# The end of the sample tile: gating ahead of the norm factor, new homes for squares and factors, new orders on three engines

## Chip, cores and metric

One core of one Trainium2 chip runs the whole program. The metric is the device time of one execution in microseconds (us), lower is better.

## The reference, cut to what matters

Two layers of a hybrid encoder run over 512 prompt tokens and 8 x 16 sample tokens with shared weights. The first layer's mixer holds four gated-DeltaNet heads and four mLSTM heads. This case is about how the outputs of the eight heads are finished and about the states of the sample sequences:

```python
o_a = o_a * lax.rsqrt(jnp.mean(o_a * o_a, axis=-1, keepdims=True) + EPS) * gdn_norm_w
o_a = o_a * jax.nn.silu(z_a)
h_b = h_b * lax.rsqrt(jnp.mean(h_b * h_b, axis=-1, keepdims=True) + EPS)
h_b = h_b * mlstm_norm_w * jax.nn.sigmoid(o_b)
out = jnp.concatenate([o_a, h_b], axis=-1) @ w_out
S = exp(gL) * S + k_end^T u            # per sequence and gated-DeltaNet head, an output
C = decay * C + kw^T v ;  n = decay * n + sum(kw)    # per sequence and mLSTM head, outputs
```

The factor of a head is 1/root of the mean of its squared output, so it has to be taken from the output before the gate (silu or sigmoid) is applied.

## The kernel before, in words

Features lie on the 128 partitions and all T = 640 tokens (512 prompt, 128 sample) on the free axis. fp32 products are made of three fp32r products, high x high, low x high and high x low, so each weight block is loaded to `raw` by SyncE, rounded to `whi` by ScalarE (`prep`) and its rest `wlo` is made by GpSimd (`low`). The mixer's core walks over five token tiles; the first four belong to the prompt, the fifth is the sample tile. Every engine has its own instruction order written out by hand, and engines meet at semaphores only, so a waiting instruction holds back all that stands behind it on its engine.

The end of the sample tile, on each engine:

- TensorE (`sample_tile` and `first_blocks`): `state_c(h)` makes the increment of the mLSTM state C of head h (4 matmuls into ps[1]); it waits for `spread_state(h)` of ScalarE and for `add_c(h-1)` of VectorE. `state_s(h)` does the same for the DeltaNet state S in ps[2]; the first waits until VectorE has updated n (`ms_dve`), a later one for `spread_correction(h)` and `add_s(h-1)`. `o_sums(0)` and `o_sums(HA)` sum the squared outputs of heads 0 to 3 and 4 to 7 over the partitions (48 matmuls by 24 rows). Then `first_blocks` moves n to rows with five transposes and starts the output projection: three blocks n, n+1, n+2 of eight k-steps each, first k = 0..3 of each (heads 0 to 3), then k = 4..7. A k-step is six 128 x 320 matmuls. Step k of block n waits for `h_ready` k+1, that is for VectorE's `low(k)`. Block n+3 follows. `unused_products` are transposes whose result nobody reads.
- ScalarE: `spread_state(h)` and `spread_correction(h)` write eight masked copies each. `spread_correction(1)` overwrites what `state_c(1)` reads, and so waits for `c_product` 2, the end of `state_c(1)`. `o_square(first)` squares four heads, `o_roots(first)` takes the root of the 24 x 128 sums (it needs another activation table), `o_cast(q)` makes the high part `hh` of a finished head.
- VectorE: `add_c(h)`, `add_s(h)` add the increments to the states; three operations finish the mLSTM outputs (maximum, reciprocal, product); two small ones update n; `inverse(i)` is the reciprocal of the 24 x 128 roots; `normalise(q)` multiplies a head by weight and factor and then by its gate z; `low(q)` makes the low part `hl`.
- SyncE: after `inverse(i)` it stores the 24 x 128 factors to `o_rows` in HBM (L977), waits for that, and loads them back broadcast over all partitions, one transfer for each of four heads (L984), into the places `o_scale(q)`. Between and behind these stand the stores of the states, each waiting for its `add_s(h)` and `add_c(h)`, and behind them the loads of the next output-projection blocks (L862).

The planes 0 to 7 of `qkv` become `hh`, the planes 8 to 15 become `hl`; until then their upper halves hold squares (`o_squares`) and factors (`o_scale`), and their lower ones gates z (`z_both`).

Of the kernel before, what the change touches and what calls it, by code (L numbers as in the profile page):

```python
# [5 lines left out]
def stream_step(nc, ins, outs):  # L6
# [44 lines left out]
    with ctx:  # L51
# [17 lines left out]
        def sem(name):  # L69
            return ctx.enter_context(nc.semaphore(name))  # L70
# [129 lines left out]
        def bank(i):  # L200
            return ps[i // 2][:, i % 2, :]
# [28 lines left out]

        def o_squares(q):

            if q < HA:
                return qkv[:, q:q + 5:4, HT:T]
            return qkv[:, q:q + 9:8, HT:T]

        def o_scale(q):

            return qkv[:, (0, 2, 8, 10, 4, 6, 12, 14)[q]:(2, 4, 10, 12, 6, 8, 14, 16)[q], HT:T]

        def norm_chunks(q, c):

# [117 lines left out]
        o_inverse = sem("o_inverse")  # L360
        o_rows_stored = sem("o_rows_stored")
        o_scale_loaded = [sem(f"o_scale_loaded{q}") for q in range(2 * HA)]
        o_gated = sem("o_gated")
        o_high = sem("o_high")
        v_spread = sem("v_spread")
        c_product = sem("c_product")
# [714 lines left out]
        def _(pe):  # L1081
# [173 lines left out]
            def unused_products(out, count):  # L1255

                for _ in range(count):
                    pe.transpose(out, ident[:], ident[:])
# [174 lines left out]
            def o_sums(first):  # L1433

                pe.wait_ge(o_squared, first + HA)
                steps = [(q, c, piece) for q in range(first, first + HA) for c in range(2) for piece in norm_chunks(q, c)]
                for i, (q, c, (off, w, row)) in enumerate(steps):
                    last = pe.matmul(bank(1 - first // HA)[0:6 * HA, 0:w], pick[:, 6 * HA - 1 - row:12 * HA - 1 - row],
                                     o_squares(q)[:, c, off:off + w], start=(i == 0), stop=(i == len(steps) - 1), skip_group_check=True)
                last.then_inc(o_summed, 1)  # L1440

            def sample_tile():
# [85 lines left out]
                sample_num(2)  # L1528
                sample_num(3)
                sample_part("den")  # L1530
                state_c(1)
                sample_part("nsum")
                o_sums(0)
                state_s(0)
                state_c(2)
                state_s(1)
                o_sums(HA)
                state_c(3)
                state_s(2)
                unused_products(bank(6)[:, 0:P], 12)  # L1540
                state_s(3)

            def first_blocks(s):
                n, (hi, lo) = s["n0"], s["hid"]

                hidden = (h_ready, s["hbase"])

                pe.wait_ge(ms_dve, MS_DVE.index("n") + 1)

                pe.wait_ge(o_root, 2)  # L1550
                pe.transpose(bank(0)[0:HB, P:2 * P], pC[:, :, P], ident[:])
                for h in range(HB):
                    last = pe.transpose(bank(1)[0:DECB, h * P:(h + 1) * P], stc[:, h, :, P], ident[:])
                last.then_inc(n_moved, 1)
                for k in range(HA):
                    mm(n, hi, lo, first=hidden, part=(k, k + 1))

                pe.wait_ge(states_done, 2)
                mm(n + 1, hi, lo, part=(0, HA))

                pe.wait_ge(c_added, HB)
                mm(n + 2, hi, lo, part=(0, HA))
                mm(n, hi, lo, first=hidden, part=(HA, KD))
                mm(n + 1, hi, lo, part=(HA, KD))

                mm(n + 2, hi, lo, part=(HA, KD))

                pe.wait_ge(s_added, HA)

            def state_c(h):  # L1570

                pe.wait_ge(v_spread, h + 1)
                if h == 0:

                    pe.wait_ge(p_kept, 1)

                    pe.wait_ge(ms_act, MS_ACT.index("kt") + 1)
                else:

                    pe.wait_ge(c_added, h)  # L1580
                for c in range(2):
                    last = pe.matmul(ps[1][:, c, :], VS(6)[:, h], spread_v(h)[:, c * 4:(c + 1) * 4, :], start=True, stop=True)
                last.then_inc(c_product, 1)
# [34 lines left out]
            def sample_part(part):  # L1618
                t = NTILE - 1
                q, k, v = (qkv[:, a:a + HB, tile(t)] for a in (8, 12, 20))  # L1620
                if part == "qk":
                    last = per_head(6, lambda h: k[:, h], lambda h: q[:, h])
                elif part == "vt":

                    pe.wait_ge(ms_dve, MS_DVE.index("qk") + 1)
                    for h in range(HB):
                        last = pe.transpose(bank(6)[:, h * P:(h + 1) * P], v[:, h], ident[:])
                elif part == "kt":

                    pe.wait_ge(ms_dve, MS_DVE.index("kend") + 1)  # L1630
                    for h in range(HB):
                        last = pe.transpose(bank(6)[:, h * P:(h + 1) * P], VS(4)[:, h], ident[:])
                elif part == "den":

                    pe.wait_ge(ms_act, MS_ACT.index("kt") + 1)
                    pe.wait_ge(ms_dve, MS_DVE.index("nq") + 1)
                    for h in range(HB):
                        hs = h * P
                        pe.matmul(bank(6)[:, hs:hs + P], one[:].to_broadcast([P, P]), VS(3)[:, h], start=True, stop=False)
                        last = pe.matmul(bank(6)[:, hs:hs + P], one[:].to_broadcast([P, P]), VS(7)[:, h], start=False, stop=True)  # L1640
                else:

                    pe.wait_ge(z_out, 4 * (NTILE - 1))
                    for h in range(HB):
                        last = pe.matmul(bank(5)[:, h * DECB:(h + 1) * DECB], VS(6)[:, h], bmask[:], start=True, stop=True)
                last.then_inc(ms_pe, 1)
# [181 lines left out]
        def _(act):  # L1828
# [207 lines left out]
            for s in stages:  # L2036
# [263 lines left out]
                elif kind == "core":  # L2300
# [169 lines left out]
                    act.wait_ge(core["utok"], t + 1)  # L2470
                    spread_correction(1)
                    o_roots(0)
                    spread_state(3)
                    o_square(HA)
                    prep(z0 + 10)
                    spread_correction(2)
                    o_roots(HA)
                    spread_correction(3)

                    def o_cast(q):  # L2480

                        if q % HA == 0:

                            act.wait_ge(o_gated, q + HA)
                        act.copy(hh[:, q, :], qkv[:, 16 + q, :]).then_inc(o_high, 1)

                    for q in range(HA):
                        o_cast(q)

                    act.wait_ge(n_moved, 1)  # L2490
                    act.copy(nout[0:HB, 0:P], bank(0)[0:HB, P:2 * P]).then_inc(states_done, 1)
                    act.copy(nout[0:DECB, P:], bank(1)[0:DECB, :]).then_inc(states_done, 1)
                    for q in range(HA, 2 * HA):
                        o_cast(q)
                elif kind == "ple":
# [58 lines left out]
        def _(dve):  # L2554
            own = Tally(dve)

            def o1(i):
                own(i.then_inc(dve_own, 1), dve_own)
# [314 lines left out]
            def sample_tile():  # L2873
# [127 lines left out]

                c1 = NV2 - 1 - HB

                def normalise(q_):
                    o = qkv[:, 16 + q_, :]
                    w_ = vec2[:, NV2 - 1:NV2] if q_ < HA else vec2[:, c1 + q_ - HA:c1 + q_ - HA + 1]

                    dve.wait_ge(o_scale_loaded[q_], 16)
                    o1(dve.scalar_tensor_tensor(halves(o), halves(o), w_, o_scale(q_), ALU.mult, ALU.mult))

                    dve.wait_ge(z_act, q_ + 1)
                    o4 = o.rearrange("p (c i j) -> p c i j", c=2, i=4)
                    own(dve.tensor_tensor(o4, o4, z_both(q_), ALU.mult).then_inc(o_gated, 1), o_gated)

                def low(q_):

# [13 lines left out]
                                      bmask[:].unsqueeze(2).to_broadcast([P, DECB, P]), ALU.mult).then_inc(u_first, 1), u_first)  # L3030
                decay_c(2)
                decay_c(3)

                dve.wait_ge(ms_act, MS_ACT.index("den") + 1)
                o1(dve.tensor_tensor(VS(0), VS(0), VS(2), ALU.max))
                o1(dve.reciprocal(VS(0), VS(0)))
                own(dve.tensor_tensor(bv, heads(7), VS(0), ALU.mult).then_inc(o_new, 1), o_new)
                add_c(1)

                dve.wait_ge(ms_pe, MS_PE.index("nsum") + 1)  # L3040
# [2 lines left out]
                ms(dve.tensor_tensor(n_, W(0)[:, :, 0:DECB], bank(5)[:, 0:HB * DECB].rearrange("p (h b) -> p h b", h=HB), ALU.add))  # L3043
                dve.sem_inc(ms_dve, 1)
                own.counts[ms_dve.name] += 1
                inverse(0)
                add_s(0)
                add_c(2)
                add_s(1)
                normalise(0)  # L3050
                normalise(1)
                inverse(1)
                normalise(2)
                add_c(3)
                add_s(2)
                normalise(3)
                low(0)
                add_s(3)
                low(1)
                low(2)  # L3060
                low(3)
                for q_ in range(HA, 2 * HA):
                    normalise(q_)
                for q_ in range(HA, 2 * HA):
                    low(q_)

            def mlstm_part(t, part):
                z = slice(t * P, (t + 1) * P)
# [587 lines left out]
```

## Time and profile before

| | us |
|---|---|
| median of 3 runs (2608.93 to 2610.06) | 2608.99 |
| profiled execution, its own time | 2611.51 |
| span of the profiled execution, first to last instruction | 2609.8 |
| TensorE busy in the span | 2564.2 |
| VectorE busy | 2105.4 |
| ScalarE busy | 1213.3 |
| GpSimd busy | 355.2 |
| mean granted TensorE clock | 0.995 |

PE is TensorE's matmuls, PEld its weight loads, DVE VectorE, ACT ScalarE, POOL GpSimd, SP SyncE (SPq its queue of transfers). Times in the trace are us from the start of the span. PEclk is the granted clock as a share of full speed; 1.00 is 2.4 GHz and 0.50 is 1.2 GHz. A line number is that of the kernel above; a helper's line stands for all who call it (L2561 is a product on VectorE, L1319 a product for each head, L1258 an unused transpose, L1109, L1110 and L1113 are a k-step). The stretch that the change touches lies between 862 and 915 us.

### The profile page before, as it was taken

The numbers are of one execution on the slowest core, as the hardware profiler recorded it, in microseconds if no ns is written. First come the engines' busy times: TensorE is split into PE (matmuls) and PEld (weight loads), VectorE is DVE, ScalarE is ACT, GpSimd is POOL, SyncE is SP. The second block draws the span as 40 slices with busy tenths as digits, with TensorE's granted clock in tenths as the row PEclk, the third lists the DMA queues.
The fourth block names the chain that finished last, engine by engine and source line by source line (L and its number), as shares of the span: only waits on it lengthen the run. The fifth ranks groups of instructions, "written<-read, shape, count | busy, mean of one in ns | idle before, by whom it ended". The sixth has DMA issues, their size and how long they took to land.

```text
span 2609.8 us, 43704 instructions
## 1 busy us (share of the span) xinstructions
PE 2564.2 (98%) x17600; PEld 2533.9 (97%) x17600; DVE 2105.4 (81%) x2614; ACT 1213.3 (46%) x1921; POOL 355.2 (14%) x186
## 2 busy tenths in 40 slices
PE   9999999998999999999999999999999999999998
PEld 9999999998999799999999999999999999999998
DVE  7979786887787889898877998988757788898756
ACT  5535454343444545455445554645311355454445
POOL 2200003332010120000024200000333300000042
PEclk9999999999999999999999999999999999999999
DMA  4223323232114423223323222223322222332231
GB/s 127 82 81 92 87 78 90 61 84 78 53 36 111 130 65 90 82 82 91 88 71 94 71 83 81 82 85 91 88 77 74 61 78 81 90 89 82 84 97 49
DMA packets 420251, 215.13 MB, mean 82 GB/s; under 512 B 19218, under 2 KB 418011, under 8 KB 420048
## 3 DMA queue, kind: packets, MB, share of 16 engines
q1 hardware_dynamic: 406066, 205.36, 27.6%
q10 hardware_dynamic: 13982, 6.96, 1.0%
q8 instruction: 140, 2.29, 0.4%
q14 instruction: 63, 0.52, 0.1%
HBM read 204.58 MB, written 7.68 MB: 81 GB/s over the span
## 4 chain that ended last, share of the span: by engine, by line
PE 56%; DVE 8%; ACT 2%; issue 1%; POOL 0%; DVEq 0%; ACTq 0%
PE ps L1124 13%; PE ps L1126 13%; PE ps L1125 13%; PE ps L1109 5%; PE ps L1110 5%; PE ps L1113 5%; PE ps L1182 1%; PE ps L1184 1%; PE ps L1183 1%; DVE sumsq L2666 1%; DVE ut L2561 1%; DVE x L3389 1%; DVE tau_lo L2630 1%; DVE r L2752 0%; DVE x L3574 0%
## 5 line engine op out<-in xcount | busy, mean ns | idle before, releaser
L1057 POOL TENSOR_TENSOR wlo<-raw,whi 128x1024 fp32r<-128x1024 f32 (+2 forms) x150 | 339.7, 2266 | 2215.9 <-ACT whi L1852 2215.9
L1124 PE MATMUL ps<-tau_hi,whi 128*128 128x320 f32 x1280 | 396.2, 309 | 0.5 <-ACT sq L2090 0.5
L1125 PE MATMUL ps<-tau_lo,whi 128*128 128x320 f32 x1280 | 395.9, 309 | 0.0
L1126 PE MATMUL ps<-tau_hi,wlo 128*128 128x320 f32 x1280 | 395.9, 309 | 0.0
L1863 ACT CAST whi<-raw 128x512 fp32r<-128x512 f32 (+4 forms) x368 | 258.1, 714 | 195.3 <-PE ps L1126 189.3
L1109 PE MATMUL ps<-xh,whi 128*128 128x320 f32 x1040 | 317.0, 313 | 4.2 <-POOL wlo L1057 2.3
L1110 PE MATMUL ps<-xl,whi 128*128 128x320 f32 x1040 | 313.4, 309 | 0.0
L2577 DVE TENSOR_TENSOR wlo<-raw,whi 128x512 fp32r<-128x512 f32 (+4 forms) x368 | 289.4, 801 | 17.3 <-ACT whi L1863 17.1
L1109 PE MATMUL ps<-hh,whi 128*128 128x320 f32 x928 | 282.4, 312 | 4.4 <-DVE hl L3018 2.1
L1110 PE MATMUL ps<-hl,whi 128*128 128x320 f32 x928 | 280.3, 310 | 0.0
L2577 DVE TENSOR_TENSOR wlo<-wsum,whi 128x1536 fp32r<-128x1536 f32 (+2 forms) x112 | 180.8, 1614 | 81.8 <-ACT whi L1863 80.3
L1124 PEld LDWEIGHTS ps<-tau_hi,whi 128*128 128x128 f32 x1280 | 240.5, 188 | 1.0 <-ACT sq L2090 1.0
L1125 PEld LDWEIGHTS ps<-tau_lo,whi 128*128 128x128 f32 x1280 | 240.4, 188 | 0.0
L1126 PEld LDWEIGHTS ps<-tau_hi,wlo 128*128 128x128 f32 x1280 | 240.4, 188 | 0.0
L1113 PE MATMUL ps<-xh,wlo 128*128 128x320 f32 x1040 | 237.2, 309 | 0.0
L1124 PE MATMUL ps<-xh,whi 128*128 128x320 f32 x724 | 224.9, 311 | 3.4 <-DVEq L2565 2.9
L1125 PE MATMUL ps<-xl,whi 128*128 128x320 f32 x724 | 224.5, 310 | 0.0
L1126 PE MATMUL ps<-xh,wlo 128*128 128x320 f32 x724 | 224.3, 310 | 0.0
L1124 PE MATMUL ps<-hh,whi 128*128 128x320 f32 x716 | 221.7, 310 | 0.9 <-DVEq L2565 0.6
L1125 PE MATMUL ps<-hl,whi 128*128 128x320 f32 x716 | 221.4, 309 | 0.0
L1126 PE MATMUL ps<-hh,wlo 128*128 128x320 f32 x716 | 221.3, 309 | 0.0
L1852 ACT CAST whi<-raw 128x1024 fp32r<-128x1024 f32 (+2 forms) x152 | 141.1, 930 | 161.4 <-PE ps L1113 150.6
(498 smaller groups left out, 6120.0 us busy)
## 6 DMA issues: line engine op xcount, KB each, us to landing
raw<-in_ffn_w_gu SPq DMA_DIRECT2D x320, 256.0 KB, 3.8
raw<-in_ffn_w_d SPq DMA_DIRECT2D x96, 192.0 KB, 3.0
raw<-in_w_in_even SPq DMA_DIRECT2D x32, 512.0 KB, 4.1
raw<-in_ffn_w_d SPq DMA_DIRECT2D x32, 384.0 KB, 3.6
raw<-in_w_in_odd SPq DMA_DIRECT2D x24, 512.0 KB, 3.8
raw<-in_ffn_w_gu SPq DMA_DIRECT2D x16, 512.0 KB, 4.3
raw<-in_ffn_w_d SPq DMA_DIRECT2D x64, 128.0 KB, 2.7
raw<-in_w_ple_gate SPq DMA_DIRECT2D x16, 512.0 KB, 4.1
```

Source lines behind the costliest of these rows:

```text
L1057: pool.tensor_tensor(ring(wlo, n), raw[:, slot, 0:kt, :], ring(whi, n).bitcast(fp32), ALU.subtract).then_inc(lo_ready, 1)
L1109: pe.matmul(ps[j % 4][:, c, 0:HT], wh[:, k], hi[:, k, cs], start=(k == 0), stop=False)
L1110: pe.matmul(ps[j % 4][:, c, 0:HT], wh[:, k], lo[:, k, cs], start=False, stop=False)
L1113: last = pe.matmul(ps[j % 4][:, c, 0:HT], wl[:, k], hi[:, k, cs], start=False, stop=(k == kt - 1))
L1124: pe.matmul(out, whi[:, w], hi(i), start=(start and i == 0), stop=False, skip_group_check=True)
L1125: pe.matmul(out, whi[:, w], lo(i), start=False, stop=False, skip_group_check=True)
L1126: last = pe.matmul(out, wlo[:, w], hi(i), start=False, stop=(i == kt - 1), skip_group_check=True)
L1182: pe.matmul(out, whi[:, w], high[:, k, cs], start=(start and k == ks[0]), stop=False, skip_group_check=True)
L1183: pe.matmul(out, whi[:, w], low[:, k, cs], start=False, stop=False, skip_group_check=True)
L1852: act.copy(ring(whi, n), raw[:, raw_pos["block", n], 0:kt, :]).then_inc(hi_ready, 1)
L1863: act.copy(group_ring(whi, p, g), group_raw(p, g)).then_inc(pair_hi, 1)
L2577: dve.tensor_tensor(group_ring(wlo, p, g), group_raw(p, g), group_ring(whi, p, g).bitcast(fp32), ALU.subtract).then_inc(pair_lo, 1)
```

## The change

On VectorE the product with z is taken out of `normalise` and becomes `gate(q)`, which runs once the head has been squared; four gates stand ahead of the first factors' arrival. `inverse(0)` moves from behind the update of n to a place ahead of `add_c(1)`. `add_s(1)` to `add_s(3)` move back, the last behind all of the heads. On TensorE `o_sums(0)` moves ahead of `state_c(1)`, `o_sums(HA)` ahead of `state_s(1)`; the five transposes of n move forward and into banks 6 and 7; twelve unused transposes go; `state_s(3)` moves between the half blocks n+1 and n+2. On ScalarE `o_square(HA)` moves ahead of `spread_state(3)`, the copies of n ahead of `o_roots(HA)`, and `prep(z0 + 10)` and `spread_correction(3)` behind the casts of heads 0 to 3; each cast waits for its own head instead of for four. SyncE's order is unchanged.

```diff
         def o_squares(q):
-            if q < HA:
-                return qkv[:, q:q + 5:4, HT:T]
-            return qkv[:, q:q + 9:8, HT:T]
+            return qkv[:, q % HA:q % HA + 5:4, HT:T]
         def o_scale(q):
-            return qkv[:, (0, 2, 8, 10, 4, 6, 12, 14)[q]:(2, 4, 10, 12, 6, 8, 14, 16)[q], HT:T]
+            a = (12, 14, 8, 10, 4, 6, 12, 14)[q]
+            return qkv[:, a:a + 2, HT:T]
...
                 sample_part("den")
+                o_sums(0)
                 state_c(1)
                 sample_part("nsum")
-                o_sums(0)
                 state_s(0)
                 state_c(2)
+                normalisers_out()
+                o_sums(HA)
                 state_s(1)
-                o_sums(HA)
                 state_c(3)
                 state_s(2)
-                unused_products(bank(6)[:, 0:P], 12)
-                state_s(3)
+
+            def normalisers_out():
+                pe.wait_ge(ms_dve, MS_DVE.index("n") + 1)
+                pe.transpose(bank(6)[0:HB, 0:P], pC[:, :, P], ident[:])
+                for h in range(HB):
+                    last = pe.transpose(bank(7)[0:DECB, h * P:(h + 1) * P], stc[:, h, :, P], ident[:])
+                last.then_inc(n_moved, 1)
             def first_blocks(s):
...
-                pe.wait_ge(ms_dve, MS_DVE.index("n") + 1)
-                pe.wait_ge(o_root, 2)
-                pe.transpose(bank(0)[0:HB, P:2 * P], pC[:, :, P], ident[:])
...
+                pe.wait_ge(states_done, 2)
                 for k in range(HA):
                     mm(n, hi, lo, first=hidden, part=(k, k + 1))
-                pe.wait_ge(states_done, 2)
+                pe.wait_ge(o_root, 2)
                 mm(n + 1, hi, lo, part=(0, HA))
+                state_s(3)
...
                     spread_correction(1)
                     o_roots(0)
+                    o_square(HA)
                     spread_state(3)
-                    o_square(HA)
-                    prep(z0 + 10)
                     spread_correction(2)
+                    act.wait_ge(n_moved, 1)
+                    act.copy(nout[0:HB, 0:P], bank(6)[0:HB, 0:P]).then_inc(states_done, 1)
+                    act.copy(nout[0:DECB, P:], bank(7)[0:DECB, :]).then_inc(states_done, 1)
                     o_roots(HA)
-                    spread_correction(3)
                     def o_cast(q):
-                        if q % HA == 0:
-                            act.wait_ge(o_gated, q + HA)
+                        act.wait_ge(o_scaled, q + 1)
                         act.copy(hh[:, q, :], qkv[:, 16 + q, :]).then_inc(o_high, 1)
                     for q in range(HA):
                         o_cast(q)
-                    act.wait_ge(n_moved, 1)
...
+                    prep(z0 + 10)
+                    spread_correction(3)
                     for q in range(HA, 2 * HA):
                         o_cast(q)
...
+                def gate(q_):
+                    dve.wait_ge(o_squared, q_ + 1)
+                    dve.wait_ge(z_act, q_ + 1)
+                    o4 = qkv[:, 16 + q_, :].rearrange("p (c i j) -> p c i j", c=2, i=4)
+                    o1(dve.tensor_tensor(o4, o4, z_both(q_), ALU.mult))
...
                 decay_c(3)
+                gate(0)
+                gate(1)
...
                 own(dve.tensor_tensor(bv, heads(7), VS(0), ALU.mult).then_inc(o_new, 1), o_new)
+                inverse(0)
+                gate(2)
+                gate(3)
                 add_c(1)
...
-                inverse(0)
                 add_s(0)
                 add_c(2)
+                for q_ in range(HA):
+                    normalise(q_)
+                gate(4)
+                inverse(1)
+                gate(5)
+                low(0)
+                low(1)
                 add_s(1)
-                normalise(0)
-                normalise(1)
-                inverse(1)
-                normalise(2)
+                low(2)
+                low(3)
                 add_c(3)
                 add_s(2)
-                normalise(3)
-                low(0)
-                add_s(3)
-                low(1)
-                low(2)
-                low(3)
+                gate(6)
+                gate(7)
                 for q_ in range(HA, 2 * HA):
                     normalise(q_)
                 for q_ in range(HA, 2 * HA):
                     low(q_)
+                add_s(3)
```

## Rows read from the trace of the kernel before

**Rows 1.** The page: busy time of the engines

```profile
PE 2564.2 (98%) x17600; PEld 2533.9 (97%) x17600; DVE 2105.4 (81%) x2614; ACT 1213.3 (46%) x1921; POOL 355.2 (14%) x186
```

**Rows 2.** Stretches: length, busy PE, PEld, DVE, ACT, POOL; PEclk, DMA share, GB/s

```profile
890.00:895.00 5.00, 3.41 (x14) 3.18 (x15) 4.79 (x7) 1.94 (x5) 0.00 (x0) 0.77 1.14 350
895.00:900.00 5.00, 5.00 (x32) 5.00 (x32) 4.79 (x7) 0.00 (x0) 0.00 (x0) 0.89 1.13 334
```

**Rows 3.** Timeline of TensorE: start, length, line, operation [idle before <- releaser]

```profile
862.14 1.88 PE L1582 MATMUL ps<-W,VS 128*128 128x512 f32 x4
863.86 0.95 PE L1645 MATMUL ps<-bmask,VS 128*128 128x8 f32 x8
864.75 4.57 PE L1438 MATMUL ps<-qkv,R 128*24 128x128 f32 x48
869.93 1.95 PE L1598 MATMUL ps<-W 128*128 128x512 f32 x4 [0.61 <-DVEq L3044]
...
887.03 1.96 PE L1598 MATMUL ps<-W 128*128 128x512 f32 x4 [2.10 <-DVE sg L2994]
...
890.50 0.38 PE L1109 MATMUL ps<-hh,whi 128*128 128x320 f32 x1 [0.96 <-DVE hl L3018]
...
892.71 0.63 PE L1109 MATMUL ps<-hh,whi 128*128 128x320 f32 x1 [1.09 <-DVE hl L3018]
...
914.55 0.31 PE L1109 MATMUL ps<-hh,whi 128*128 128x320 f32 x1
```

**Rows 4.** Timeline of ScalarE

```profile
864.12 2.45 ACT L2400 ACTIVATE W<-W,bmask 128x128 f32<-128x128 f32 x8 [0.25 <-PE ps L1582]
866.59 1.28 ACT L2415 ACT_TABLE_LOAD   x1
869.35 0.36 ACT L2415 ACTIVATE VS<-ps,eps 24x128 f32<-24x128 f32 x1 [1.48 <-PE ps L1438]
...
913.53 1.03 ACT L1852 CAST whi<-raw 128x1024 fp32r<-128x1024 f32 x1
```

**Rows 5.** Timeline of VectorE

```profile
863.04 0.69 DVE L3035 TENSOR_TENSOR VS<-VS 128x512 f32<-128x512 f32 x1 [1.28 <-ACT VS L2467]
...
867.16 0.69 DVE L3037 TENSOR_TENSOR qkv<-ps,VS 128x512 f32<-128x512 f32 x1
867.88 1.41 DVE L2986 TENSOR_TENSOR stc<-stc,ps 128x512 f32<-128x512 f32 x2
...
869.93 0.94 DVE L3000 RECIPROCAL VS<-VS 24x128 f32<-24x128 f32 x1
...
879.50 0.89 DVE L3009 SCALAR_TENSOR_TENSOR qkv<-qkv,vec 128x640 f32<-128x640 f32 x1
880.42 0.82 DVE L3013 TENSOR_TENSOR qkv<-qkv,sumsq 128x640 f32<-128x640 f32 x1
...
889.52 0.82 DVE L3018 TENSOR_TENSOR hl<-qkv,hh 128x640 fp32r<-128x640 f32 x1 [0.86 <-ACT hh L2485]
```

**Rows 6.** Timeline of TensorE where the core of the mixer starts

```profile
641.70 2.08 PE L1319 MATMUL ps<-W,qkv 128*128 128x128 f32 x8 [6.32 <-DVE W L2779]
```

**Rows 7.** A stretch of TensorE alone: length, busy; PEclk, DMA share, GB/s

```profile
646.00:648.00 2.00, 2.00 (x12) 0.78 0.00 0
```

**Rows 8.** Timeline of SyncE's queue

```profile
872.22 1.90 SPq L984 DMA_DIRECT2D qkv<-o_rows  x4
...
898.29 16.09 SPq L862 DMA_DIRECT2D raw<-in_w_out_even  x4
```

**Rows 9.** Transfers of L984, then of L862 into output blocks, from issue to landing

```profile
DMA to landing us min/median/max: 3.4/5.5/6.1
...
DMA to landing us min/median/max: 3.8/5.5/9.7
```

**Rows 10.** Timeline of ScalarE at another table load

```profile
835.66 1.28 ACT L2446 ACT_TABLE_LOAD   x1
836.95 0.74 ACT L2446 ACTIVATE qcopy<-qcopy 128x640 f32<-128x640 f32 x1
```

More of the change, by code:

```diff
@@ L362, in stream_step @@
         o_scale_loaded = [sem(f"o_scale_loaded{q}") for q in range(2 * HA)]
-        o_gated = sem("o_gated")
+        o_scaled = sem("o_scaled")
         o_high = sem("o_high")
@@ L1546, in first_blocks @@
                 hidden = (h_ready, s["hbase"])
-                pe.wait_ge(ms_dve, MS_DVE.index("n") + 1)
-                pe.wait_ge(o_root, 2)
-                pe.transpose(bank(0)[0:HB, P:2 * P], pC[:, :, P], ident[:])
-                for h in range(HB):
-                    last = pe.transpose(bank(1)[0:DECB, h * P:(h + 1) * P], stc[:, h, :, P], ident[:])
-                last.then_inc(n_moved, 1)
+                pe.wait_ge(states_done, 2)
                 for k in range(HA):
                     mm(n, hi, lo, first=hidden, part=(k, k + 1))
-                pe.wait_ge(states_done, 2)
+                pe.wait_ge(o_root, 2)
                 mm(n + 1, hi, lo, part=(0, HA))
+                state_s(3)
                 pe.wait_ge(c_added, HB)
@@ L2488, in _ @@
                         o_cast(q)
-                    act.wait_ge(n_moved, 1)
-                    act.copy(nout[0:HB, 0:P], bank(0)[0:HB, P:2 * P]).then_inc(states_done, 1)
-                    act.copy(nout[0:DECB, P:], bank(1)[0:DECB, :]).then_inc(states_done, 1)
+                    prep(z0 + 10)
+                    spread_correction(3)
                     for q in range(HA, 2 * HA):
@@ L3008, in normalise @@
                     dve.wait_ge(o_scale_loaded[q_], 16)
[L3009 to L3013, printed above, removed]
+                    own(dve.scalar_tensor_tensor(halves(o), halves(o), w_, o_scale(q_), ALU.mult, ALU.mult).then_inc(o_scaled, 1), o_scaled)
                 def low(q_):
```

## The prediction

> **What bounds the kernel now.** I read the page first: TensorE is busy 2564.2 of 2609.8 us [rows 1], so an edit is worth what it takes from TensorE's remaining waits, or adds to them. The stretches around the changed code come next: from 890 to 900 us TensorE lacks 1.6 us of work and is granted 0.77 and 0.89 of its clock [rows 2]. Its timeline then shows what it waits for [rows 3]: 2.10 us for `add_s(2)` ahead of `state_s(3)`, then 0.96 and 1.09 us for `low(0)` and `low(1)`. From 914.55 on, where block n+3 starts, TensorE runs through, so that time is the mark against which I sum: whatever shifts it shifts the end. ScalarE and VectorE are read over the same stretch [rows 4, 5]; VectorE, hardly ever idle there, sets the pace.
>
> **The first part: one engine's order against another's.** Three moves act together. I follow them from 862.14, where `state_c(1)` starts now; nothing earlier changes.
>
> TensorE: `o_sums(0)` (4.55 us) now goes first, 862.1 to 866.7; its squares are ready, as they stand on ScalarE ahead of the earlier `den` copy. `state_c(1)` (1.75) ends at 868.5 instead of 863.9, the sum over tokens (0.9) at 869.3 [rows 3].
>
> ScalarE: `spread_correction(1)` waits for the end of `state_c(1)`, and `o_roots(0)` stands behind it. So the correction (2.45) runs from 868.5 to 871.0 instead of from 864.12. Then come the table load (1.28) and the root (0.36), which ends at 872.6, against 869.7 before [rows 4]. The sums come 2.6 us sooner, and their root 2.9 us later.
>
> VectorE: `gate(0)` and `gate(1)` fall into the idle 1.28 us ahead of the maximum (2 x 0.85, so everything to the mLSTM product is 0.45 us late, its end at 868.3). Then it stands at `inverse(0)` until 872.7: 4.4 us idle. Behind it are the reciprocal (0.97), gates 2 and 3 (1.73), `add_c(1)` (1.45) and n (0.5), so n is ready at 877.3 [rows 5]. `state_s(0)` waits for n: it starts at 877.4 instead of 869.93, and TensorE has been idle for 8.1 us.
>
> **The clock on top.** After an idle 6.32 us, TensorE restarted at 641.70 [rows 6] and had its full clock back within the stretch 646 to 648, of which a share of 0.78 means half speed until about 647.1 [rows 7]: some 5.4 us at 1.2 GHz after the restart. I expect the same until 882.7: `state_s(0)` takes 3.6 us, `state_c(2)` 2.6, together 2.7 us more than at full speed. The cost is bounded below by nothing and above by half of 5.4; I take the upper end, as the wait is longer than that at 641.70.
>
> **From there to the mark.** VectorE: `add_s(0)`, `add_c(2)` from 883.7 to 885.2; four normalisations without gate (4 x 0.93) to 888.9; gate 4, `inverse(1)`, gate 5 (0.86 + 0.98 + 0.86) to 891.6; `low(0)`, `low(1)` to 893.3; `add_s(1)` to 894.8. The factors of heads 0 to 3 are no wait: their loads went out 1.3 us behind `inverse(0)`, over 1.9 us, and took 6.1 us to land at most [rows 5, 8, 9], so they are all there by 883. TensorE: n's transposes, `o_sums(HA)`, `state_s(1)` and `state_c(3)` (0.65 + 4.55 + 1.8 + 1.8) end at 892.4. `state_s(2)` has to wait for `add_s(1)`, which now stands behind two lows: 2.4 us idle, then 894.8 to 896.6. ScalarE's casts have been done since about 892, so the k-steps run without a wait: 24 x 0.88 = 21.1 us, and `state_s(3)` inside them, 1.8. Sum: 896.6 + 21.1 + 1.8 = 919.5.
>
> Two corrections. The same chaining of the old order gave 0.3 us too little up to 877, so I add 0.3. The new wait of 2.4 us may bring a second slow stretch, as the old ones did (0.23 x 5 + 0.11 x 5 = 1.7 us, [rows 2]): between 0 and 1.7, and I take 0.9, as the three old waits (4.2 us) were more. That is 920.7, or 6.2 us behind 914.55.
>
> **What is gained and is in this sum already.** The twelve unused transposes (1.4 us) lay in a wait, and go for nothing. The waits of 2.10, 0.96 and 1.09 us and the old slow stretch go, about 5.8 us; in their place come 8.1 and 2.4 us of waits, 2.7 us of slow clock and the 0.9. The gates move work and don't add any: 0.89 + 0.82 before and after for each head [rows 5].
>
> **What costs nothing.** `prep(z0 + 10)` moves behind the casts: on ScalarE at about 892 to 893, GpSimd 2.4 us behind it, so its block is ready at 896 and needed at 905.5. Were that cover gone, each us would count. `spread_correction(3)` follows at 893 to 896, needed at 903.7. `low(4)` ends at about 905.9 and is needed at 909.1. On SyncE the state stores and the next weights wait for `add_s(3)`, now the last work on VectorE, at about 909.8. The loads of block n+4 go out near 913 instead of 898.29; with the longest landing of such a load, 9.7 us, it is there at 922.7, and with the median at 918.5 [rows 8, 9]. ScalarE's cast of it stood at 913.53 [rows 4] and comes at 919.7; TensorE needs it by 927.7, less 3.4 us for cast and rest. So it is hidden by 1.6 us at worst.
>
> **A rule against a row.** The root's table load is followed at once by its activation where nothing else is awaited: 835.66 + 1.28, next start 836.95 [rows 10]; I have used that. The Trainium skill, "ScalarE: Activation LUTs", section "What ACT_TABLE_LOAD costs", adds a drain of some 1.38 us to every switch. The row does not show it. By that page the root would end at 874.0 and the estimate would be 1.4 us higher.
>
> **Rivals.**
> - ScalarE is not held (the other side). If the root came by 868.3, when VectorE reaches `inverse(0)`, n would be ready at 873.0, the wait of TensorE would shrink to 3.8 us, and the mark would come 4.4 us sooner, less up to 1.8 of slow clock: 914 to 916, so 2608.5 to 2610.5, not slower. It turns on whether `state_c(1)` ends before the correction is reached at about 864; for it speaks only that the sums are ready at 866.7, against it that `state_c(1)` stands behind them. 8%. A true gain of over 5 us would need the second wait gone as well: 4%.
> - The same chain with little slow clock (it falls elsewhere, or later parts absorb some): mark at 917 to 919.7, so 2611.5 to 2614.2. 24%.
> - The late weights. If the state stores hold the loads of n+4 back beyond 924.4, each us counts: 3 us more would give 2618.2. For it: 1 MB of stores stands directly ahead. 5%.
> - The drain after the table load, above, as a mechanism of this kernel: root 1.4 us later, 2616.6. 5%.
> - My forecast, the chain with its slow clock: 54%.
>
> **How the numbers follow.** The profiled execution has its own 2611.51 with a span of 2609.8; the median of runs is 2608.99, and as the difference lies in profiling, I add the 6.2 us to the median: 2615.2. The range leaves out the first rival and what exceeds 3 us more: 2611.4 to 2618.6. A measurement of this kernel can tell about 0.2%, or 5.2 us, from no change; 6.2 is little above that. Slower by more: most of the forecast case (50%), the drain and the late weights (10%), 60% in all; within: the small-clock rival, the first one and the low end of the forecast (24 + 8 + 4 = 36%); faster: 4%.
>
> **What would show it.** Right: VectorE idle some 4 us ahead of the 24 x 128 reciprocal with the root of ScalarE as its releaser; the root at 872 to 873 behind the correction at 868.5; TensorE idle about 8 us ahead of `state_s(0)` and a clock of 0.5 from then to about 883; no waits between k-steps; block n+3 near 920.7. Wrong: the root before 869, or `state_s(0)` before 873. The late half is wrong if a k-step waits for a low, if a wait stands ahead of block n+3 or n+4, or if `state_s(2)` doesn't wait for `add_s(1)`.

## The result and the profile after

The changed kernel takes 2620.88 us (median of 8 executions, 2613.95 to 2621.95). Eight of the kernel before, the three of the table above and five taken beside the changed kernel, have a median of 2612.17, and the ratio is 1.0031 with a 95% interval of 1.0021 to 1.0040: slower by 5.5 to 10.4 us. A second measurement gave 1.0025 (1.0016 to 1.0035). The sign and the size of the difference (forecast 6.2 us) hold; the forecast time of 2615.2 with its upper end of 2618.6 does not.

The profiled execution is the fastest of the eight (2613.95, span 2612.2). It reached the end of `den` (the last sums over partitions ahead of the change) 2.3 us earlier than the profiled execution of the kernel before, so I compare from there on. TensorE after (start, length, line, operation, idle before and releaser):

```profile
859.59 0.39 PE L1642 MATMUL ps<-VS,one 128*128 128x128 f32 x2
859.91 4.57 PE L1437 MATMUL ps<-qkv,R 128*24 128x128 f32 x48
864.41 1.98 PE L1584 MATMUL ps<-W,VS 128*128 128x512 f32 x4
866.23 0.95 PE L1647 MATMUL ps<-bmask,VS 128*128 128x8 f32 x8
875.45 3.75 PE L1600 MATMUL ps<-W 128*128 128x512 f32 x4 [8.27 <-DVEq L3054]
879.00 2.78 PE L1584 MATMUL ps<-spread_c,VS 128*128 128x512 f32 x4
...
892.98 1.95 PE L1600 MATMUL ps<-W 128*128 128x512 f32 x4 [2.52 <-DVE sg L2995]
894.37 0.71 PE L1108 MATMUL ps<-hh,whi 128*128 128x320 f32 x1
...
917.83 0.38 PE L1108 MATMUL ps<-hh,whi 128*128 128x320 f32 x1
```

Against [rows 3]: the first line is the end of `den`; from 0.27 us behind its start (859.86, taken in the same way in every trace) to the start of block n+3 it is 57.97 us, where it was 52.36. `state_s(0)` waits 8.27 us for n instead of 0.61, and then takes 3.75 us instead of 1.95. The three waits of 2.10, 0.96 and 1.09 us are gone; one of 2.52 us ahead of `state_s(2)` stands in their place. The k-steps from 894.37 on run without a wait. The clock in the same trace (length and busy of TensorE; PEclk, DMA share, GB/s):

```profile
865.00:870.00 5.00, 2.18 (x12) 1.00 0.00 0
870.00:875.00 5.00, 0.00 (x0) 0.56 0.14 41
875.00:880.00 5.00, 4.55 (x6) 0.50 0.73 227
880.00:885.00 5.00, 5.00 (x39) 0.92 0.66 194
```

TensorE falls to 1.2 GHz during its wait and is back at 2.4 GHz only at about 881. ScalarE after:

```profile
866.49 2.45 ACT L2402 ACTIVATE W<-W,bmask 128x128 f32<-128x128 f32 x8 [4.94 <-PE ps L1584]
868.96 1.28 ACT L2417 ACT_TABLE_LOAD   x1
870.25 0.36 ACT L2417 ACTIVATE VS<-ps,eps 24x128 f32<-24x128 f32 x1
```

It stands 4.94 us for `state_c(1)`, which is now behind `o_sums(0)`; the sums have been ready since 864.4, and the root comes at 870.6. VectorE after:

```profile
865.30 0.69 DVE L3044 TENSOR_TENSOR qkv<-ps,VS 128x512 f32<-128x512 f32 x1
870.71 0.94 DVE L3001 RECIPROCAL VS<-VS 24x128 f32<-24x128 f32 x1 [4.72 <-ACT VS L2417]
...
913.99 0.49 DVE L2665 COPY sumsq<-qcopy 128x640 f32<-128x640 f32 x1 [2.32 <-DMA out_mlstm_n_s<-nout]
```

The reciprocal waits 4.72 us for the root (it waited for nothing in [rows 5]). The last line is a wait that my prediction does not have: behind the first block's x update, VectorE waits until all state stores have landed, as their place is about to be overwritten. SyncE's queue after shows why they are late, behind the last `add_s(3)`:

```profile
908.34 0.37 SPq L989 DMA_DIRECT2D out_gdn_S_s<-sg  x1
...
911.88 6.20 SPq L861 DMA_DIRECT2D raw<-in_w_out_even  x4
```

### The profile page after: what moved, and what is told of

Its sections match the earlier page's. It is cut to its first block, busy times and chain, and to the rows that moved or that the text cites. A ratio compares the mean times of both kernels' runs of the same rounds, so it can differ in the third digit from the quotient of the medians.

```text
span 2612.2 us, 43680 instructions
## 1 busy us (share of the span) xinstructions
PE 2561.2 (98%) x17588; PEld 2529.4 (97%) x17588; DVE 2104.6 (81%) x2614; ACT 1213.9 (46%) x1921; POOL 357.1 (14%) x186
## 4 chain that ended last, share of the span: by engine, by line
PE 56%; DVE 8%; ACT 2%; issue 1%; DMA 0%; SPq 0%; POOL 0%; DVEq 0%; ACTq 0%
PE ps L1123 13%; PE ps L1125 13%; PE ps L1124 12%; PE ps L1108 5%; PE ps L1112 4%; PE ps L1109 4%; PE ps L1181 1%; PE ps L1183 1%; PE ps L1182 1%; DVE sumsq L2667 1%; DVE ut L2562 1%; DVE x L3400 1%; DVE tau_row L2615 1%; DVE tau_lo L2631 1%; DVE r L2753 0%
```

## The experiments

Each kernel is the changed one with the edit shown, but for before_sums_first and before_again, which are made from the kernel before. "Stretch" is the time from the end of `den`, as above, to block n+3 in one trace; ratios are to executions of the kernel before that belong to the same measurement.

| kernel | stretch, us | median, us | ratio (95%) |
|---|---|---|---|
| before | 52.36, 52.40 | 2611.57 to 2612.17 | 1 |
| changed | 57.97, 59.44 | 2620.88, 2617.77 | 1.0031 (1.0021 to 1.0040), 1.0025 (1.0016 to 1.0035) |
| root_first | 53.76 | 2614.10 | 1.0007 (0.9998 to 1.0015) |
| sums_late | 55.92 | 2617.16 | 1.0014 (1.0005 to 1.0023) |
| adds_early | 57.63 | 2618.33 | 1.0025 (1.0015 to 1.0036) |
| fill | 57.81 | 2616.67 | 1.0015 (1.0006 to 1.0024) |
| inverse_late | 56.84 | 2616.29 | 1.0016 (1.0007 to 1.0025) |
| before_sums_first | 55.62 | 2614.56 | 1.0008 (0.9998 to 1.0017) |
| add_s3_early | 59.00 | 2618.01 | 1.0024 (1.0014 to 1.0033) |
| root_add_s3 | 54.94 | 2613.96 | 1.0013 (1.0004 to 1.0021) |
| reordered | 46.89 | 2609.28 | 0.9985 (0.9976 to 0.9994) |
| reordered_2 | 47.01 | 2606.47 | 0.9979 (0.9970 to 0.9989) |

**again**, the changed kernel with no edit.

> The changed kernel once more. Theory A (the stall chain: VectorE waits for a root that stands behind spread_correction(1), TensorE waits for n, and its clock falls): against the kernel before on the same chip 5.5 to 8.5 us more; in the trace VectorE idle 4.5 to 4.9 us ahead of the first 24 x 128 reciprocal, TensorE idle about 8.2 us ahead of state_s(0), and from the end of the last den matmul to block n+3 57.9 us where no second slow stretch falls behind it and up to 59.6 where one does (the kernel before: 52.4). Theory B (the loss lies in the late half, the stores and the weights behind add_s(3)): waits ahead of blocks n+3 or n+4. Theory C (chance: slow stretches of TensorE elsewhere differ between executions): the difference to the kernel before is within 2 us.

The ratio means 6.5 us (4.2 to 9.1). The trace repeats the waits of 8.27 and 2.53 us. The stretch is 1.5 us longer, as TensorE's clock was low from 855 on, with 0.67 and 0.78 of it granted in these two stretches; `o_sums(0)` took 5.47 us instead of 4.57:

```profile
855.00:862.00 7.00, 7.00 (x48) 0.67 0.00 0
862.00:867.00 5.00, 5.00 (x44) 0.78 0.00 0
```

**root_first** takes out one edge of the chain.

```diff
-                    spread_correction(1)
                     o_roots(0)
+                    spread_correction(1)
```

> The root taken ahead of spread_correction(1) on ScalarE, nothing else changed. Theory A: VectorE finds the root ready, its 4.7 us wait goes; TensorE's wait ahead of state_s(0) falls from 8.2 to about 3.8 us, and the whole is 4 to 5.5 us faster than the changed kernel, so within 3 us of the kernel before. Theory B: no more than 1 us faster than the changed kernel.

VectorE's wait falls from 4.72 to 0.32 us, TensorE's from 8.27 to 3.88 (timelines of VectorE and TensorE):

```profile
866.23 0.94 DVE L3001 RECIPROCAL VS<-VS 24x128 f32<-24x128 f32 x1 [0.32 <-ACT VS L2417]
```

```profile
870.97 3.75 PE L1600 MATMUL ps<-W 128*128 128x512 f32 x4 [3.88 <-DVEq L3054]
...
929.76 0.39 PE L1108 MATMUL ps<-hh,whi 128*128 128x320 f32 x1 [1.98 <-POOL wlo L1056]
```

The stretch is 4.2 us shorter, and by the ratios the whole is 4.7 us faster than in again (the intervals do not overlap). This swap of two lines gives back most of the loss. But a new wait of 1.98 us stands two blocks behind n+3, for a weight's low part; it led to theory D, below.

**sums_late** restores TensorE's old order at the head.

```diff
-                o_sums(0)
                 state_c(1)
                 sample_part("nsum")
+                o_sums(0)
```

> o_sums(0) back behind state_c(1) and the sum for n on TensorE, as in the kernel before; VectorE keeps the new order. Theory A: state_c(1) and the correction are early again, the root comes at the end of o_sums(0) plus 0.4 us, some 3 us sooner than in the changed kernel; VectorE still waits about 1.5 us for it; 2.5 to 3.5 us faster than the changed kernel. Theory B: unchanged.

Timelines of VectorE and TensorE:

```profile
873.58 0.94 DVE L3001 RECIPROCAL VS<-VS 24x128 f32<-24x128 f32 x1 [1.50 <-ACT VS L2417]
```

```profile
878.32 3.75 PE L1600 MATMUL ps<-W 128*128 128x512 f32 x4 [5.24 <-DVEq L3054]
```

VectorE's wait is 1.50 us, TensorE's 5.24, and the stretch 2.1 us shorter than the changed kernel's, though a second slow stretch of the clock falls into it. By the ratios the whole is 2.9 us faster than again, as theory A has it; these two intervals overlap.

**adds_early**

```diff
                 for q_ in range(HA):
                     normalise(q_)
+                add_s(1)
                 gate(4)
                 inverse(1)
                 gate(5)
                 low(0)
                 low(1)
-                add_s(1)
```

> add_s(1) ahead of gate(4), inverse(1), gate(5), low(0) and low(1) instead of behind them. Theory A: the second wait of TensorE, 2.5 us ahead of state_s(2), goes, and low(0) comes 1.5 us later, in front of nothing; 1.5 to 2.2 us faster than the changed kernel. Theory B (late half decides): the same or more, up to 4 us.

A miss for both. The wait ahead of `state_s(2)` went, and came back as long ahead of the first k-step (timeline of TensorE):

```profile
892.25 1.96 PE L1600 MATMUL ps<-W 128*128 128x512 f32 x4
896.86 0.38 PE L1108 MATMUL ps<-hh,whi 128*128 128x320 f32 x1 [2.65 <-DVE hl L3023]
```

`state_s(2)` and the first k-step need `add_s(1)` and `low(0)`, and VectorE has all its work ahead of the later of the two in either order. That late wait does not hang on the order of these two; in reordered, below, gates 4 and 5 stand behind both, and it falls to 1.30 us. And here the wait for the stores, 4.78 us on VectorE, reached TensorE, as 2.25 us for a weight's low part behind block n+3; a part of any gain may have gone there.

**fill** keeps TensorE busy in its wait.

```diff
                 sample_part("nsum")
+                unused_products(bank(0)[:, 0:P], 60)
                 state_s(0)
```

> The changed kernel with 60 unused transposes on TensorE in its long wait ahead of state_s(0) (some 7 us of work by the rows of the others). They delay nothing. The clock's share of theory A: no slow stretch after the wait, state_s(0) and state_c(2) take 1.9 us each instead of 3.75 and 2.8; den to n+3 2.5 us less, about 55.3. If the clock costs nothing there, 57.9 stays.

```profile
870.42 6.75 PE L1257 MATMUL ps<-ident 128*128 128x128 f32 x60
878.84 1.95 PE L1601 MATMUL ps<-W 128*128 128x512 f32 x4 [1.67 <-DVEq L3055]
880.63 1.88 PE L1585 MATMUL ps<-spread_c,VS 128*128 128x512 f32 x4
```

`state_s(0)` and `state_c(2)` take 1.95 and 1.88 us instead of 3.75 and 2.78: 2.7 us of the chain is clock. The stretch, 57.81, does not show it at once. In this execution the clock was low in the early `o_sums(0)` (5.44 us), as in again, and once more from `state_s(2)` on (2.51 us instead of 1.96, the first k-steps with it), as in neither trace of the changed kernel. Against again the stretch is 1.6 us shorter, with some 1.7 us lost in that second slow stretch (a granted clock of 0.66 from 895 to 900). The ratio, 1.0015, is 2.6 us under again's, with intervals that overlap.

**inverse_late**

```diff
-                inverse(0)
                 gate(2)
                 gate(3)
                 add_c(1)
...
                 own.counts[ms_dve.name] += 1
+                inverse(0)
                 add_s(0)
```

> inverse(0) behind n's update on VectorE again; ScalarE and TensorE keep the new orders, so the root is as late as in the changed kernel (12.5 us behind the last den matmul). Theory A: the root no longer stands ahead of n; VectorE's wait falls away or to 1 us, TensorE's ahead of state_s(0) from 8.2 to 4 to 5 us; den to n+3 about 54, 4 us faster than the changed kernel. If the late root itself is what costs (the factors come late and hold the heads up), no gain over 1 us.

Only half of it came. n is early, TensorE's first wait falls to 2.61 us; but the root is as late as in the changed kernel, and now the factors are awaited. Timelines of TensorE and VectorE:

```profile
889.75 3.75 PE L1600 MATMUL ps<-W 128*128 128x512 f32 x4 [6.04 <-DVE sg L2995]
```

```profile
878.07 3.65 DVE L3018 SCALAR_TENSOR_TENSOR qkv<-qkv,vec 128x640 f32<-128x640 f32 x4 [1.52 <-DMA qkv<-o_rows]
...
884.45 3.71 DVE L3023 TENSOR_TENSOR hl<-qkv,hh 128x640 fp32r<-128x640 f32 x2
```

Normalising waits 1.52 us for the transfer from `o_rows`, and the two lows take 3.71 us instead of 1.68, beside GpSimd (last section). These 3.5 us are what TensorE's wait ahead of `state_s(2)` has grown by, from 2.52 to 6.04. So the late root costs in two ways, through n and through the factors, and the lows met GpSimd's work on a weight. The stretch is 1.1 us shorter, and the ratios give 2.4 us back, with intervals that overlap, where 4 were expected.

**before_sums_first**: the kernel before with the one move on TensorE that sums_late takes back.

> The kernel before with the one move of o_sums(0) ahead of state_c(1) on TensorE, none on the other engines. Theory A: the root comes 3 us later although its sums are 2.6 us earlier, n's update is 4.5 us later as the sum for n stands behind o_sums(0) and add_c(1) behind state_c(1); den to n+3 2 to 4 us more than 52.4. If the squares' sum wants to be early, faster by 1 us or more.

The stretch is 3.2 us longer than the kernel before's, by the ratio the whole 2.1 us (not clear of noise by itself). VectorE waited 2.24 us for the root there, behind n. So in the trace TensorE's move alone loses, and with `inverse(0)` ahead of n, in the changed kernel, VectorE's wait is 4.72 us and holds n as well.

**add_s3_early** and **root_add_s3** take the late stores back, in the changed kernel and in root_first.

```diff
                 for q_ in range(HA, 2 * HA):
                     normalise(q_)
+                add_s(3)
                 for q_ in range(HA, 2 * HA):
                     low(q_)
-                add_s(3)
```

> The changed kernel with add_s(3) ahead of low(4) instead of behind low(7), so the last state store goes out some 3 us earlier. In the traces so far VectorE waits 2.3 us for the stores ahead of the first sum of squares, and TensorE does not feel it. Theory D (it is felt in other executions): the whole 1 us or more faster than the changed kernel. Theory A alone: VectorE's wait goes or falls below 0.5 us, den to n+3 stays at 57.9 to 59.4, the whole within 1 us of the changed kernel.

> Both: the root ahead of spread_correction(1), and add_s(3) ahead of low(4). With the root alone TensorE waited 1.98 us for a weight's low part two blocks behind block n+3, after VectorE had stood 2.9 us for the stores. Theory D (late stores hold VectorE, VectorE holds ScalarE's casts, these hold TensorE): that wait goes, the whole about 2 us faster than with the root alone, so about the kernel before. If the wait has another cause it stays.

In both VectorE's wait for the stores is gone. In the changed kernel it brings nothing (1.0024), so its wait of 2.3 us is hidden: theory D falls for it. In root_add_s3 TensorE's wait of 1.98 us is gone from the trace, and from block n+3 to the end it is 1695.0 us where root_first had 1698.0. But its stretch is 1.2 us longer, with a second slow stretch of the clock in it, and the measured ratio is 1.0013 where root_first had 1.0007, with intervals that overlap: the expected gain of 2 us is not shown.

**reordered** and **reordered_2** keep the early gates and the new homes, and order the rest by the chain found. The line in parentheses stands for the lines that update n.

```diff
                 o_sums(0)
-                state_c(1)
                 sample_part("nsum")
+                state_c(1)
...
-                    spread_correction(1)
+                    spread_state(3)
                     o_roots(0)
                     o_square(HA)
-                    spread_state(3)
+                    spread_correction(1)
                     spread_correction(2)
...
+                (n's update)
                 inverse(0)
-                gate(2)
-                gate(3)
                 add_c(1)
-                (n's update)
+                gate(2)
                 add_s(0)
+                gate(3)
                 add_c(2)
                 for q_ in range(HA):
                     normalise(q_)
-                gate(4)
-                inverse(1)
-                gate(5)
                 low(0)
-                low(1)
                 add_s(1)
+                inverse(1)
+                low(1)
                 low(2)
                 low(3)
-                add_c(3)
                 add_s(2)
+                gate(4)
+                gate(5)
+                add_c(3)
                 gate(6)
```

> A version made after the stall theory: the gate ahead of the norm and the new homes are kept; the sum for n goes ahead of state_c(1) on TensorE and n's update ahead of inverse(0) on VectorE; ScalarE takes spread_state(3) and the root ahead of the corrections; add_s(1) and add_s(2) come between the lows. Theory A: TensorE and VectorE have no wait over 1 us between the last den matmul and block n+3, no slow stretch falls there; den to n+3 in 45 to 47 us against 52.4 of the kernel before, 5 to 7 us faster than it. Theory C (what is measured is mostly slow clock elsewhere): within 2 us of it.

The stretch is 46.89 us, 5.5 less than before. The largest wait of TensorE in it is 1.30 us, VectorE's largest for the factors 1.05 us (over the 1 us expected), and no slow clock falls there. The whole is 3.9 us faster than the kernel before, less than the 5 to 7 expected. The rest was lost behind block n+3: from there to the end it is 1697.2 us against 1695.3 and 1694.7 in the traces of the kernel before. There the wait for the stores did reach TensorE. Timelines of VectorE, ScalarE, GpSimd and TensorE:

```profile
908.70 0.49 DVE L2665 COPY sumsq<-qcopy 128x640 f32<-128x640 f32 x1 [5.34 <-DMA out_mlstm_n_s<-nout]
```

```profile
911.00 0.74 ACT L1906 ACTIVATE stt<-x 128x640 f32<-128x640 f32 x1 [4.76 <-DVE x L3401]
...
918.90 0.74 ACT L1906 ACTIVATE qcopy<-x 128x640 f32<-128x640 f32 x1 [5.50 <-DVE x L3401]
...
921.87 1.05 ACT L1854 CAST whi<-raw 128x1024 fp32r<-128x1024 f32 x1
```

```profile
923.00 2.78 POOL L1056 TENSOR_TENSOR wlo<-raw,whi 128x1024 fp32r<-128x1024 f32 x1 [7.09 <-ACT whi L1854]
```

```profile
925.92 0.38 PE L1108 MATMUL ps<-hh,whi 128*128 128x320 f32 x1 [2.49 <-POOL wlo L1056]
```

The same edit that sends the stores earlier also sends the loads of the next weights earlier, so late weights are the rival of theory D. These rows speak against it: ScalarE stands for VectorE's x updates, its cast of the weight follows its other work without a wait for a load, GpSimd stands for that cast, and TensorE for GpSimd.

reordered_2 moves `add_s(3)` ahead of `low(4)` as above, and gates 4 and 5 around `normalise(0)`, into VectorE's waits for factors.

```diff
+                gate(4)
                 normalise(0)
+                gate(5)
...
                 add_s(2)
-                gate(4)
-                gate(5)
                 add_c(3)
```

> The reordered version with add_s(3) ahead of low(4), and gates 4 and 5 in the gaps in which VectorE waited 0.35 and 1.05 us for factors. Theory D: VectorE's 5.3 us wait for the stores falls to 2 us or less, TensorE's 2.5 us wait for a weight two blocks behind n+3 goes; den to n+3 46 to 48 us; 2 us faster than the reordered version, 6 us faster than the kernel before.

```profile
904.13 0.49 DVE L2665 COPY sumsq<-qcopy 128x640 f32<-128x640 f32 x1 [0.88 <-ACT qcopy L1906]
```

The stores' wait is gone, TensorE's 2.49 us too, and the ratio is 0.9979 (0.9970 to 0.9989): 5.5 us under the kernel before, and by the ratios some 14 under the changed one's first measurement and 12 under its second. The two versions' intervals overlap, so that the second is the faster rests on the traces.

**before_again**, for the second trace of the kernel before.

> The kernel before once more, for a second trace. From the last den matmul to block n+3 52.4 us, or some 1.7 us less where no slow stretch falls into the k-steps; no wait of VectorE for the state stores.

The stretch is 52.40 us with a slow stretch of the clock at the first k-steps, as before. The end of `den` lay at 859.56, not 862.19, and this one execution took 2608.44. So of the 3.1 us between this execution and the one profiled first, 2.6 had arisen ahead of everything that the change touches.

## Why the prediction was right and wrong

**The chain** came as worked out, each term within 0.4 us, counted from the end of `den`: VectorE's wait 4.72 (4.4), TensorE's 8.27 (8.1), `state_s(0)` and `state_c(2)` 3.75 and 2.78 (3.6 and 2.6), the wait ahead of `state_s(2)` 2.52 (2.4), no wait between k-steps. root_first shows that the root's place on ScalarE is the cause of most of it, sums_late and before_sums_first by their traces that TensorE's move makes it late, fill what the clock adds (2.7 us, as taken at its upper end).

The prediction's list of what is gained and lost does not add up to its 6.2: 8.1 + 2.4 + 2.7 + 0.9 less 5.8 is 8.3. It leaves out 2.1 us that go as well, the wait of 0.61 ahead of `state_s(0)` and the twelve transposes (1.47). With them the measured terms close: 8.27 + 2.52 + 2.7 less 0.61, 2.10, 0.96, 1.09, 1.47 and 1.7 is 5.6, and the stretch grew from 52.36 to 57.97. The forecast itself was summed along the chain and does not suffer from it.

**The second slow stretch**, 0.9 us as a mean of 0 and 1.7, came in neither trace of the changed kernel between 892 and 900, so the sum was 57.7 (from 862.14 to 919.8) + 0.9 where the trace has 57.97. It did come in sums_late, fill and root_add_s3. That 6.2 us in all fits so well is in part luck: this term was a mean of two cases, and the 5.6 and 7.0 us by which the two stretches grew lie around it. In again a slow stretch fell ahead of the wait, on `o_sums(0)`.

**The step that failed** is the last one, the level to which the difference is added: "as the difference lies in profiling, I add the 6.2 us to the median". The premise is wrong. The profiled 2611.51 is the usual time of the kernel before: its median is 2612.17 beside the changed kernel and 2611.57 to 2612.0 over the 24 to 33 executions of each later measurement, which lie between 2608.3 and 2615.4. It is the three executions behind 2608.99 that lie at the fast end of the spread, and no more than chance put them there as far as the runs show. Nor does profiling add time elsewhere: the profiled execution of the changed kernel is the fastest of its eight (2613.95), that of sums_late the slowest of its eleven, with one other (2618.83). Added to 2611.51 the 6.2 us would have given 2617.7, added to 2612.17 2618.4. The term mis-sized is thus the level, by 3.2 us. The other 2.5 us to 2620.88 lie within the interval (5.5 to 10.4), and the second measurement has 6.5. Whether a part of them is real stays open.

What moves the level is not in the change: the end of `den`, up to which TensorE's order is the same in all kernels here, lay between 859.56 and 865.96 us. The level goes with the granted clock. Of 86 executions of the kernel before beside the experiments, those with a mean clock of 0.994 took 2615.1 us on average, with 0.995 2611.8 and with 0.996 2609.2. Why one execution meets more slow stretches than another stays open.

**What costs nothing.** `prep(z0 + 10)`, `spread_correction(3)`, the late lows and the late weights were hidden in the changed kernel, as said. But of the late stores I named only the weights queued behind them. That VectorE itself waits for them, behind the first x update, was missed; in the changed kernel it is hidden, in root_first, adds_early and reordered it reached TensorE.

**The rivals.** The root behind the drain of the Trainium skill ("ScalarE: Activation LUTs", "What ACT_TABLE_LOAD costs") did not show: 868.96 + 1.28, next start 870.25, with the sums ready since 864.4. "ScalarE is not held" fell with its 4.94 us wait. As root_first it was made true, and gave the price that the rival had: mark 4.4 us sooner, measured 4.2. The slow clock that the rival might have saved (up to 1.8 us) stayed.

## What to carry to other kernels

Where several engines follow orders written by hand, an operation moved forward on one engine has to be followed through what stands between its result and the next user's queue: here 4.55 us of sums went ahead of four matmuls that another engine's copy waited for, with the wanted root behind that copy. A long wait of the busiest engine can cost twice, once as idle time and once in that engine's clock after it: here 8.27 us and then 2.7. And a forecast of a few us should be given as a difference first, since the level of three executions can be 3 us off; the profiled execution is one more sample of that level.

## What had not been expected of the hardware

VectorE's lows beside GpSimd: two in a row took 3.71 us in inverse_late while GpSimd worked on a weight from 883.99 on for 2.62 us, and 1.68 us without it. In the kernel before, two additions that read a PSUM bank kept their 1.41 us beside GpSimd (875.61, GpSimd from 875.57). The Trainium skill, "GPSIMD Engine Reference", section "1. Specifications", says that GpSimd shares its SBUF interfaces with VectorE and contends with its instructions that have two SBUF inputs. The rows agree, and give the size: 2 us for this pair, and as much for a single operation of 0.89 us in root_first (2.92 us from 911.04 on, GpSimd from 910.55 on for 2.73). In both cases that is about what GpSimd still had to do when VectorE's operation began (2.2 us).

The clock of TensorE after its 8.27 us wait stayed at 1.2 GHz for 5.4 us of work (to 880.8), and for 6.1 us after a wait of 3.88 us (root_first): `state_s(0)` 3.75 and `state_c(2)` 3.20 us. So halving the wait gave nothing back in the clock. In reordered the waits stayed at or under 1.30 us, and the clock at 2.4 GHz up to block n+3; but in before_sums_first a wait of 1.36 us was followed by a slow stretch (`state_s(0)` 2.54 us instead of 1.95), so the length of the wait alone does not tell.
